# Early expert units in split form during the picking, 26 instead of 23 of them before the first table group

## What is computed

```python
q = (ht @ w_q).reshape(n_tok, 8, 256)
s1 = einsum('thd,kd->thk', q[..., :128], sub_keys[0])
s2 = einsum('thd,kd->thk', q[..., 128:], sub_keys[1])
v1, i1 = top_k(s1, 16);  v2, i2 = top_k(s2, 16)
cand = v1[..., :, None] + v2[..., None, :]          # 16 x 16 sums per token and head
top, pos = top_k(cand, 16)                          # 16 experts per token and head
gate = softmax(top)
act = gelu(einsum('td,thkd->thk', h, expert_u[eidx]))
y = einsum('thk,thkd->td', gate * act, expert_v[eidx])
```

## Time and profile before

| | us |
|---|---|
| median of 3 runs | 2464.11 |
| lowest to highest | 2463.63 to 2464.44 |
| the profiled execution's own time | 2463.14 |
| its span in the trace | 2461.3 |

### The profile page before, as it was taken

How to read it: one execution, slowest core, us unless ns; L and a number is a source line. 1 busy time by engine, 2 the same in 40 slices (tenths; PEclk the granted TensorE clock), 3 DMA queues, 4 the chain that set the end, 5 groups by cost and what they waited for, 6 DMA issues and landing times. The chain is left out here.

```text
span 2461.3 us, 36638 instructions
## 1 busy us (share of the span) xinstructions
PE 2364.9 (96%) x14280; PEld 2123.6 (86%) x14280; DVE 1797.1 (73%) x2913; ACT 1157.5 (47%) x1707; POOL 148.3 (6%) x141
## 2 busy tenths in 40 slices
PE   4979999999999999999999999999999999999998
PEld 4879898888888888889899888888888888898998
DVE  7979997677667676678999676566767576555665
ACT  4542255444545454564135444455545523544554
POOL 0000153000000000000045100000000000000000
PEclk9989999999999999999999999999999999999999
DMA  9365544787676666434544586665555523343553
GB/s 356 134 227 163 157 124 149 267 298 240 233 242 231 239 231 223 148 111 139 177 135 125 188 299 220 204 216 187 189 188 191 191 78 108 124 148 126 189 186 107
DMA packets 133554, 460.63 MB, mean 187 GB/s; under 512 B 15152, under 2 KB 16432, under 8 KB 132912
## 3 DMA queue, kind: packets, MB, share of 16 engines
q1 hardware_dynamic: 133424, 458.90, 55.1%
HBM read 445.73 MB, written 13.11 MB: 186 GB/s over the span
## 5 line engine op out<-in xcount | busy, mean ns | idle before, releaser
L1654 DVE TENSOR_TENSOR ring_lo<-ring,ring_hi 128x1024 fp32r<-128x1024 f32 x421 | 506.9, 1222 | 88.6 <-ACT ring_hi L1557 88.6
L1557 ACT ACTIVATE ring_hi<-ring 128x1024 fp32r<-128x1024 f32 x421 | 435.0, 1054 | 134.0 <-PE banks L346 119.9
L319 PE MATMUL banks<-normed_lo,ring_hi 128*128 128x512 f32 x1344 | 477.9, 398 | 0.0
L344 PE MATMUL banks<-ring_hi,work_lo 128*128 128x512 f32 x1024 | 400.5, 391 | 8.0 <-DVE work_lo L1681 4.3
L345 PE MATMUL banks<-ring_lo,work_lo 128*128 128x512 f32 x1024 | 399.9, 391 | 0.0
L346 PE MATMUL banks<-ring_hi,work_lo 128*128 128x512 f32 x1024 | 399.1, 390 | 0.0
L320 PE MATMUL banks<-normed_lo,ring_lo 128*128 128x256 f32 x1344 | 377.2, 281 | 0.0
L319 PEld LDWEIGHTS banks<-normed_lo,ring_hi 128*128 128x128 f32 x1344 | 252.5, 188 | 61.8
L361 DVE TENSOR_TENSOR ring_lo<-ring,ring_hi 128x1024 fp32r<-128x1024 f32 x185 | 225.0, 1222 | 78.1 <-ACT ring_hi L356 77.5
L320 PEld LDWEIGHTS banks<-normed_lo,ring_lo 128*128 128x128 f32 x1344 | 253.8, 189 | 3.3
L1677 DVE TENSOR_TENSOR work<-banks,work 128x512 f32<-128x512 f32 x84 | 58.1, 692 | 249.2 <-ACT work L1563 249.2
(11 more groups left out here) (387 smaller groups left out, 4357.4 us busy)
## 6 DMA issues: line engine op xcount, KB each, us to landing
ring<-wstream SPq DMA_DIRECT2D x716, 512.0 KB, 3.3
arena<-wstream SPq DMA_DIRECT2D x96, 512.0 KB, 5.7
spill<-one_hots SPq DMA_DIRECT2D x44, 256.0 KB, 4.2
rstd<-spill SPq DMA_DIRECT2D x16, 256.0 KB, 4.1
pool_and_keys<-spill SPq DMA_DIRECT2D x14, 256.0 KB, 4.1
routes<-spill SPq DMA_DIRECT2D x14, 256.0 KB, 4.8
residual<-xT SPq DMA_DIRECT2D x1, 1024.0 KB, 7.8
arena<-mixconst SPq DMA_DIRECT2D x2, 512.0 KB, 4.2
```

Source lines behind the costliest of these rows:

```text
L319: pe.matmul(dst, w_hi[:, o], HR[:, k, :], start=(k == 0), stop=(k == KD - 1), skip_group_check=True)
L344: pe.matmul(dst, hi[:, t], w_hi[:, o], start=first, stop=False)
L1557: sc.activation(RING_HI[:, u % HIGHS, :], RING[:, u % SLOTS, :], ACT.Copy)\
L1654: dve.tensor_tensor(RING_LO[:, u % SLOTS, :], RING[:, u % SLOTS, :], RING_HI[:, u % HIGHS, :].bitcast(F32), ALU.subtract).then_inc(S("spli ...
```

## The change

Of the early units, numbers 2 to 16 (the third to the seventeenth of the layer) take the split form during the picking. ACT makes their high parts in the three RING_HI slots that the one-hots will use later, POOL makes the low parts, and PE waits for the low part of each unit. The first three high parts stand before the first gelu; the high part of the unit after that in the same slot stands in the step of the pair that frees it, ahead of that pair's gelu. 25 instead of 22 units run before the transposes of the routes, and one more after them, so that 18 instead of 21 are left to the table stage. ACT's fixed order becomes pairs 0 to 5, "centred" and the exponential, pairs 6 to 9, `by_tile(0)`, pairs 10 and 11, `by_tile(1)` and `by_tile(2)`.

```diff
-AHEAD_PICK = 11
+PICKED = 25
+EARLY = tuple(range(2, 17))
...
-            E0 = S_EXP + 2 * AHEAD_PICK + 1
-            N_SPLIT = 2 * (AHEAD - AHEAD_PICK) - 1
+            E0 = S_EXP + PICKED + 1
+            N_SPLIT = 2 * AHEAD - PICKED - 1
...
+            def early_slot(u):
+
+                return RING_HI[:, slot_of[EARLY.index(u - S_EXP) % HOTS], :]
...
-                                    if u < E0:
+                                    if u - S_EXP in EARLY:
+                                        if k == 0:
+                                            pe.wait_ge(S("early_low"), EARLY.index(u - S_EXP) + 1)
+                                        w_hi = early_slot(u)[:, o]
+                                        pe.matmul(dst, w_hi, H_HI[:, k, :], start=(k == 0), stop=False)
+                                        pe.matmul(dst, w_hi, H_LO[:, k, :], start=False, stop=False)
+                                        mm = pe.matmul(dst, RING_LO[:, u % SLOTS, o], H_HI[:, k, :],
+                                                       start=False, stop=(k == KD - 1))
+                                    elif u < E0:
...
-                    for _ in range(2 * KD * AHEAD_PICK):
+                    for _ in range(KD * PICKED):
                         next(first)
...
+                    def pooled_high(m):
+
+                        u = S_EXP + EARLY[m]
+                        arrived(sc, u)
+                        if m >= HOTS:
+                            sc.wait_ge(units_used, used(S_EXP + EARLY[m - HOTS]))
+                        act.mark(sc.activation(early_slot(u), RING[:, u % SLOTS, :], ACT.Copy), "pooled_high")
+
+                    def ahead_step(p):
+
+                        for m in range(HOTS, len(EARLY)):
+                            if EARLY[m - HOTS] // 2 == p:
+                                pooled_high(m)
+                        ahead_gelu(p)
+
+                    for m in range(HOTS):
+                        pooled_high(m)
                     for p in range(6):
-                        ahead_gelu(p)
+                        ahead_step(p)
                     act.wait("centred", 1)
                     act(sc.activation(GT, GT, ACT.Exp), "gate_exp")
-                    for p in range(6, 9):
-                        ahead_gelu(p)
+                    for p in range(6, 10):
+                        ahead_step(p)
                     by_tile(0, SEL[:, 0, :])
-                    for p in range(9, AHEAD_PICK):
-                        ahead_gelu(p)
+                    for p in range(10, PICKED // 2):
+                        ahead_step(p)
...
-                    p = AHEAD_PICK
+                    p = PICKED // 2
...
-                        if KD + ahead_by(g) >= 2 * KD * (p + 1 - AHEAD_PICK):
+                        if KD * (PICKED + 1) + ahead_by(g) >= 2 * KD * (p + 1):
...
                 @block.gpsimd
                 def _(pool):
+                    for m, n in enumerate(EARLY):
+                        u = S_EXP + n
+                        pool.wait_ge(S("pooled_high"), m + 1)
+                        pool.tensor_tensor(RING_LO[:, u % SLOTS, :], RING[:, u % SLOTS, :], early_slot(u).bitcast(F32),
+                                           ALU.subtract).then_inc(S("early_low"), 1)
```

## The result

The changed kernel takes 2486.43 us (median of 6 runs, 2483.4 to 2494.2) against 2463.87 of the kernel before in the same series: ratio 1.0095, 95% interval 1.0079 to 1.011. It is slower by 23 us; 2483.7 was forecast, with a range of 2467 to 2492. The profiled execution took 2487.37 us, its span is 2485.6.

A forecast was written before the change was run, and what follows sets the result against it. PE's pace was taken as the time, with PE and DVE ending the picking together. 15.4 - 8.6 + 3.0 = 9.8 us a layer, 19.6 in both, gave 2483.7; forecast's own range 2475 to 2491, overall range 2467 to 2492.

The forecast's parts named there:

- PE and DVE end the picking together: Picking before the change: PE's 22 units just fill it, DVE's last copy ending 0.5 us after them.
- The wait for "centred" in front of the high parts of units 15 and 16: ACT's order: these high parts stand behind that wait, so PE idles some 10 us ahead of unit 15.
- Unit 15: Picking, first layer: PE wants it at 258.2 but runs it from 268.2 to 271.1.
- POOL's pass: POOL's low-part subtraction over 1024 elements in the picking: taken as 2.0 us, bounds 1.04 and 3.9.
- POOL and DVE take turns: Behind "centred": L1409 to 266.1, POOL to 268.1, L1412 to 272.5, POOL's second pass to 274.5.
- Rival 1: Behind "centred": POOL isn't held up by DVE's long operations; 1.9 us a layer, 2467.9; chance 0.15.
- rival 4: Between L1409 and L1412 POOL wins the ports twice in a row: 2477 to 2480; inside the forecast's 0.67.
- The sorts: DVE's sorts in the picking: one-input instructions, so they and POOL would leave each other alone; no row shows them together.
- Rival 3: DVE's second sort collides with POOL's eight passes, "centred" up to 16 us later: up to 2516; chance 0.08.
- The half clock: After PE's idle ahead of unit 15: half clock for some 3.5 us, 1.8 us, hidden before unit 16.
- The first table: After the picking's transposes: the next unit starts at 306.1 against 290.66, 15.4 us later.
- The table stage: Three units fewer save 8.6 us; waits for the gelu, high part, low part chain cost 3.0, bounds 0 and 5.6.

The follow-up runs named there:

- experiment 5: Changed kernel with pair 6's step ahead of the wait for 'centred' and 22 instead of 25 units before the transposes: 2468.35 us, ratio 1.0017.
- experiment 6: Changed kernel with no unit in split form during the picking, still 25 units before the transposes: 2474.57 us, ratio 1.0036.
- experiment 7: Changed kernel, pair 6's step ahead of 'centred', units 5 and 6 in full form, unit 7's high part after DVE's sums: 2462.33 us, ratio 0.9992.
- experiments 3: Changed kernel with, in the table stage, ACT's high part of the unit after next made before the pair's gelu: 2485.83 us, ratio 1.0092.
- experiment 4: Changed kernel with pair 6's step ahead of 'centred' and, in the table stage, the high part before the gelu: 2463.55 us, ratio 1.0001.
- experiment 9: Against experiment 1: DVE's table-stage subtraction cut to 64 of 1024 columns, PE reading high parts for low: 2457.72 us (one run; before, same chip, 2462.2).
- experiment 1: Changed kernel with the whole step of pair 6 ahead of ACT's wait for 'centred': 2463.53 us, ratio 1.0003.
- experiment 2: Changed kernel with the picking's comparison reading its second input, the numbers 0 to 15, from PSUM instead of SBUF: 2481.08 us, ratio 1.0073.
- experiment 8: As experiment 7, with 24 instead of 25 units before the transposes: 2460.57 us, ratio 0.9984.
- experiment 10: As experiment 7, plus units 17 and 18 in split form and the comparison's second input in PSUM: 2455.66 us, ratio 0.9974.

## Why the prediction was right, step by step

- **PE and DVE end the picking together**: shown by experiment 5. PE gets 15 cheaper units and DVE's end is what counts; experiment 6 shows the other side, where three more full units bring the first table 9.3 us later.
- **A split unit saves 0.57 us**: experiment 7 is 7.5 us a layer below experiment 6, for 13 units: 0.58 each.
- **The wait for "centred" in front of the high parts of units 15 and 16**: shown. Moving that step removes the 8.22 and the 1.20 us and, of the total's loss against the kernel before, all but 0.3 us. PE's wait was 8.2 us and not 10, because it came to unit 15 later (2.1 us at unit 6 and a half clock behind it); the end of the wait isn't moved by that. ACT's wait before the exponential was 6.16 us and not about 11: PE and so the gelu before it came later, and a high part of 1.06 us (254.40) and a table load of 1.28 us (255.96) stand in that time.
- **Unit 15**: I had PE start it at 268.2, which is 269.9 with this execution's start 1.7 us later; it was 271.15. Two terms were short: the meeting with the cast (L1433), 0.9, and POOL's pass, 0.4. I had looked for operations with two SBUF inputs only, and had written that those with one keep their time beside POOL; the cast has one and was held, 1.96 us for 0.43. "Centred" came 1.5 us later relative to the start, not 0.6, and the cast's own meeting is all of it: L1435 keeps its 4.43.
- **POOL's pass**: 2.40 us, not 2.0. Twice the 1.04 us of the row for 512 elements was already too little; that row's second input is a broadcast, this one's isn't, which may be the reason but wasn't tested.
- **POOL and DVE take turns** (DVE, POOL, DVE, POOL), L1448 stretched to 6.4: it reads 6.45. By the rule of the Trainium skill ("SBUF — State Buffer", section "SBUF: two separate sides"), that the loser is blocked for a whole instruction, this was to be expected, and the trace agrees: 12.53 us for two passes of 2.40. Rival 1, in which POOL runs through, is excluded by these rows, and so is rival 4, in which POOL goes twice in a row. The same section of the Trainium skill names operations in a two-port mode as well, which would explain why the cast was held. That the cast was held the rows show; that it runs in such a mode is read only from its pace: casts of 256 and 512 elements take 0.29 and 0.43 us, 0.55 ns for each element more, where L1409 takes 4.43 us for 4096, 1.08 ns each.
- **The sorts** kept their length beside POOL: the sixteen MAX8 over the sums take 5.32 us beside POOL's run of passes (228.73 to 239.89), 5.33 before. Rival 3 falls.
- **The half clock**: granted 0.50 when unit 15 came and hidden behind the wait for unit 16, as predicted; unit 15 took 5.3 us, where 2.9 and 1.8 were allowed. What I left out is the wait at unit 6, 2.11 us and not 0.9, which could drop the clock as well (below), for 1.4 us.
- **The first table**: 15.4 us later was forecast, 16.5 measured: 0.9 more for the cast, 0.4 more for POOL's second pass, less 0.2 in what follows.
- **The table stage**: 8.6 less 3.0 was forecast, 4.4 measured. The size was near by luck, since the reason was wrong: I had the chain gelu, high part, low part as the limit, in the cycles with a gelu alone; experiments 3 and 4 refute it, and experiment 9 shows that the stage is 6.1 us a layer shorter with DVE's subtractions cut.
- **The sum**: 9.8 a layer forecast, 12.1 measured, 1.1 of the difference in the picking and 1.2 in the stage. The loss in the picking, the larger term, was forecast for the reason that the runs show. One sum in the prediction doesn't come out: with a table wait of 5.6 its terms give 15.4 - 8.6 + 5.6 = 12.4 a layer, so 2489 as the forecast's upper end and not 2491; the measured time lies below both.

## What to carry to other kernels

An engine's hand-written order is a list of waits: when work is put behind an existing wait that was free, ask when the new work is due, not when the old was. Moving work to POOL isn't free for DVE: lay the pass where DVE sorts or reads PSUM, not beside its operations with two SBUF inputs, nor, as read here for one line, beside its cast. And time saved on one engine is worth nothing where another ends at the same time; here the change paid only once PE and DVE were both relieved.

## What was unexpected

**Short waits and the granted clock.** The same wait of 2.11 us at unit 6 dropped the clock in the second layer of experiment 1 and not in the first (84.2 and 85.7 us to the first table; in experiment 4 the other way round). In the seven profiles that have this wait the granted clock fell to 0.50 within 1.2 us of its end in 9 of 14 cases, and in the other 5 it didn't fall. Experiment 1, second layer (columns as in the earlier trace rows):
```profile
1189.00:1190.00 1.00, 0.85 (x7) 0.88 (x8) 1.00 (x4) 0.00 (x0) 1.00 (x2) 0.92 0.90 258
1190.00:1191.00 1.00, 1.00 (x6) 1.00 (x6) 1.00 (x4) 0.00 (x0) 1.00 (x1) 0.50 0.89 348
...
1193.00:1194.00 1.00, 1.00 (x9) 1.00 (x9) 1.00 (x7) 0.16 (x1) 0.68 (x1) 0.87 0.00 0
```
**Parts that nobody changed.** Outside the two layer stretches the profiled span is 2054.6 us in the kernel before, 2054.8 in the changed one, 2052.0 in experiment 1, 2060.8 in experiment 2, 2059.8 in experiment 7, 2061.9 in experiment 8 and 2053.9 in experiment 10, with the same number of matmuls there. The same stretch behind the second layer, kernel before, then experiment 2:
```profile
1986.00:1991.00 5.00, 5.00 (x32) 4.61 (x32) 2.70 (x7) 0.22 (x1) 0.00 (x0) 1.00 0.18 72
```
```profile
1998.00:2003.00 5.00, 5.00 (x22) 4.46 (x22) 1.20 (x5) 0.22 (x1) 0.00 (x0) 0.57 0.17 66
```
PE is busy for all 5.00 us in both, and the granted clock is 1.00 in one and 0.57 in the other: 22 matmuls fall into the window instead of 32. So a change of a few us is to be judged by the stage that it touches: experiment 8 wins 6 us there and 4 in the total (2460.57 against 2464.79 of the kernel before on the same chip). What decides whether the clock falls there was not found.
